# A ring of nine weight slots in place of six in the expert stage of a two-layer decoder trunk

## The reference

```python
def swiglu(x, w_gate, w_up, w_down):
    return (jax.nn.silu(x @ w_gate) * (x @ w_up)) @ w_down

def moe_swiglu(xn, w_router, we_gate, we_up, we_down):
    logits = (xn @ w_router).astype(jnp.float32)
    top_v, top_i = lax.top_k(logits, TOP_K)            # TOP_K = 2
    top_w = jax.nn.softmax(top_v, axis=-1)
    gates = jnp.sum(jax.nn.one_hot(top_i, N_EXPERTS, dtype=jnp.float32) * top_w[..., None], axis=-2)
    y = jnp.zeros_like(xn)
    for e in range(N_EXPERTS):                         # 8
        y = y + gates[..., e:e + 1].astype(xn.dtype) * swiglu(xn, we_gate[e], we_up[e], we_down[e])
    return y
```

## Time and profile before

| | us |
|---|---|
| median of 3 runs (range) | 1408.41 (1406.65 to 1410.0) |
| profiled execution, whole | 1407.37 |
| its span | 1405.5 |
| TensorE matmul busy | 1325.4 (94%) |
| VectorE busy | 779.1 (55%) |
| ScalarE busy | 680.1 (48%) |
| mean granted TensorE clock | 0.994 of full |
| moved by DMA | 442.34 MB, mean 315 GB/s |
| in the chain that ended last: TensorE / DMA | 66% / 25% |

### The profile page before, as it was taken

How to read it: one execution, slowest core, us unless ns; L and a number is a source line. 1 busy time by engine, 2 the same in 40 slices (tenths; PEclk the granted TensorE clock), 3 DMA queues, 4 the chain that set the end, 5 groups by cost and what they waited for, 6 DMA issues and landing times.

```text
span 1405.5 us, 18008 instructions
## 1 busy us (share of the span) xinstructions
PE 1325.4 (94%) x6371; PEld 904.1 (64%) x6371; DVE 779.1 (55%) x1123; ACT 680.1 (48%) x941; POOL 40.4 (3%) x109
## 2 busy tenths in 40 slices
PE   9999999999999999998889998889999889999886
PEld 8998888888897878841258871137884126886112
DVE  6968655544589699910069950029991006995100
ACT  6766544444479487710068850028871006874000
POOL 1000000000010000000000000000000000000000
PEclk9999999999999999999999999999999999999999
DMA  8654565555162599989999999999999999999997
GB/s 293 191 186 157 181 201 181 190 188 195 52 230 82 206 352 403 371 315 409 402 403 409 402 348 401 407 402 406 409 402 340 409 402 403 409 402 342 404 407 297
DMA packets 150198, 442.34 MB, mean 315 GB/s; under 512 B 15486, under 2 KB 27868, under 8 KB 150108
## 3 DMA queue, kind: packets, MB, share of 16 engines
q1 hardware_dynamic: 146796, 429.92, 81.0%
q0 software_dynamic: 3280, 11.27, 2.6%
q10 hardware_dynamic: 32, 0.01, 0.0%
HBM read 434.06 MB, written 7.08 MB: 314 GB/s over the span
## 4 chain that ended last, share of the span: by engine, by line
PE 66%; DMA 25%; DVE 5%; ACT 2%; issue 1%; SPq 0%; POOL 0%; DVEq 0%; ACTq 0%; POOLq 0%
PE bank L618 62%; DMA raw<-in_we_down_dram 10%; DMA raw<-in_we_gate_dram 8%; DMA raw<-in_we_up_dram 7%; DVE w_lo L2142 3%; DVE qkT L2265 1%; PE bank L1263 1%; ACT w_hi L1534 1%; SPq L391 0%; PE bank L963 0%; PE bank L630 0%; DVE xT_lo L2186 0%; ACT xr L1669 0%; PE bank L638 0%; PE bank L1227 0%
## 5 line engine op out<-in xcount | busy, mean ns | idle before, releaser
L2142 DVE TENSOR_TENSOR w_lo<-raw,w_hi 128x1024 fp32r<-128x1024 f32 (+3 forms) x496 | 565.4, 1182 | 136.3 <-ACT w_hi L1534 131.6
L1534 ACT ACTIVATE w_hi<-raw 128x1024 fp32r<-128x1024 f32 (+3 forms) x496 | 498.5, 1032 | 199.2 <-PE bank L618 153.5
L618 PE MATMUL bank<-w_hi,xT_hi 128*128 128x512 f32 (+4 forms) x910 | 351.7, 387 | 11.0 <-DVE w_lo L2142 9.6
L618 PE MATMUL bank<-w_hi,xT_lo 128*128 128x512 f32 (+4 forms) x910 | 346.4, 381 | 0.0
L618 PE MATMUL bank<-w_lo,xT_hi 128*128 128x512 f32 (+4 forms) x910 | 346.2, 380 | 0.0
L618 PE MATMUL bank<-raw,x_half 128*64 128x512 f32 (+1 forms) x1024 | 229.2, 561 | 34.9 <-DMA raw<-in_we_gate_dram 19.7
L618 PEld LDWEIGHTS bank<-w_hi,xT_hi 128*128 128x128 f32 x910 | 171.3, 188 | 47.8 <-issue 14.7
L2911 DVE SCALAR_TENSOR_TENSOR act_f<-bank,gslot,silu_g 128x512 f32<-128x512 f32 (+1 forms) x16 | 11.0, 684 | 331.4 <-PE bank L618 331.4
L618 PEld LDWEIGHTS bank<-w_hi,xT_lo 128*128 128x128 f32 x910 | 171.3, 188 | 31.4
L618 PEld LDWEIGHTS bank<-w_lo,xT_hi 128*128 128x128 f32 x910 | 171.5, 188 | 29.2
L618 PEld LDWEIGHTS bank<-raw,x_half 128*64 128x64 f32 x1024 | 60.5, 136 | 193.2 <-DMA raw<-in_we_gate_dram 72.6
(11 more groups left out here) (407 smaller groups left out, 813.5 us busy)
## 6 DMA issues: line engine op xcount, KB each, us to landing
raw<-in_we_gate_dram SPq DMA_DIRECT2D x224, 512.0 KB, 11.8
raw<-in_we_up_dram SPq DMA_DIRECT2D x224, 512.0 KB, 12.1
raw<-in_we_down_dram SPq DMA_DIRECT2D x224, 512.0 KB, 12.3
raw<-in_w_gate_dram SPq DMA_DIRECT2D x28, 512.0 KB, 4.3
raw<-in_w_up_dram SPq DMA_DIRECT2D x28, 512.0 KB, 4.3
raw<-in_w_down_dram SPq DMA_DIRECT2D x28, 512.0 KB, 4.0
raw<-in_w_in_dram SPq DMA_DIRECT2D x32, 384.0 KB, 4.8
raw<-in_w_out_dram SPq DMA_DIRECT2D x16, 512.0 KB, 5.5
```

The costliest lines, as they stand in the source:

```text
L618: return pe.matmul(o, a, b, start=start, stop=stop, skip_group_check=True, **kw)
L1534: act.activation(split_piece(w_hi, c, shape, half), raw_piece(c, shape, half), ACT.Copy).then_inc(hi_ready, 1)
L2142: dve.tensor_tensor(split_piece(w_lo, c, shape, half), raw_piece(c, shape, half), F(split_piece(w_hi, c, shape, half)), ALU.subtract).then ...
```

## The change

`RING = 9` slots serve the expert stage. Six of them are those of `raw`. Two more (`spare`) lie above the other buffers of the stage, and the ninth (`late_slot`) where `xT_lo` lay, which is now closed before the expert stage. The two parts of a wide unit's tokens both go into `xT_hi` (`xE`): the high part in the first half of its bytes, the low part in the second. The layers before the experts keep their ring of six.

A chunk that falls into one of the three new slots is fetched by one DMA of 1 MiB (`ring_piece` with `half=None`), which waits until both halves of the chunk before it in that slot are done with; both of its pieces count as landed only with the whole. In the first lap the two `spare` slots wait for the attention scores (`scores_psum`), the late one for TensorE's last product of the output projection (`piece_used` at 2*C_MOE).

```diff
+RING = 9
@@
-        xT_lo = sb("xT_lo", [P, KD, S], F32R)
...
+        before_moe = ExitStack()
+        xT_lo = sb("xT_lo", [P, KD, S], F32R, scope=before_moe)
...
+        before_moe.close()
         part = ExitStack()
         with part:
+            late_slot = sb("late_slot", [P, CHUNK], scope=part)
...
+            spare = sb("spare", [P, 2, CHUNK], scope=part)
@@
+        def place(u, c):
+            return divmod(c - C_MOE + FFN_CHUNKS * u, RING)
+        def ring_piece(u, c, shape, half):
+            s = place(u, c)[1]
+            slot = (raw[:, (C_MOE + s) % RAW_SLOTS, :] if s < RAW_SLOTS else
+                    spare[:, s - RAW_SLOTS, :] if s < RING - 1 else late_slot[:, :])
+            k0, nk = (0, shape[0]) if half is None else pieces_of(shape)[half]
+            return slot[:, k0 * shape[1]:(k0 + nk) * shape[1]].rearrange("p (k n) -> p k n", k=nk)
+        def ring_here(u, c, half):
+            lap, s = place(u, c)
+            if s < RAW_SLOTS:
+                return raw_here[2 * ((C_MOE + s) % RAW_SLOTS) + half], 16 * ((C_MOE + s) // RAW_SLOTS + 1 + lap)
+            return spare_here[s - RAW_SLOTS], 16 * (2 + lap)
@@
             def slot_free(u, c, half):
-                owner = u if c - RAW_SLOTS >= C_MOE else u - 1
-                n = 2 * (c - RAW_SLOTS + FFN_CHUNKS * u) + half + 1
-                if owner in NARROW_UNITS:
-                    sp.wait_ge(piece_used, n)
+                lap, s = place(u, c)
+                if lap:
+                    owner, i = divmod(RING * (lap - 1) + s, FFN_CHUNKS)
+                    if owner in NARROW_UNITS:
+                        sp.wait_ge(piece_used, 2 * (C_MOE + FFN_CHUNKS * owner + i) + half + 1)
+                    else:
+                        sp.wait_ge(lo_ready, 2 * (C_MOE + split_chunks(owner) + i) + half + 1)
+                elif s < RAW_SLOTS:
+                    sp.wait_ge(lo_ready, 2 * (c - RAW_SLOTS) + half + 1)
+                elif s < RING - 1:
+                    sp.wait_ge(sem("scores_psum"), AH)
                 else:
-                    sp.wait_ge(lo_ready, n - 2 * FFN_CHUNKS * (max(owner, 0) - wides_before(owner)))
+                    sp.wait_ge(piece_used, 2 * C_MOE)
+            def fetch_expert(u, c, shape, src):
+                s = place(u, c)[1]
+                if s < RAW_SLOTS:
+                    for half, (k0, nk) in enumerate(pieces_of(shape)):
+                        slot_free(u, c, half)
+                        sp.dma_start(ring_piece(u, c, shape, half), src[:, k0:k0 + nk, :]).then_inc(
+                            raw_here[2 * ((C_MOE + s) % RAW_SLOTS) + half], 16)
+                else:
+                    slot_free(u, c, 1)
+                    sp.dma_start(ring_piece(u, c, shape, None), src).then_inc(spare_here[s - RAW_SLOTS], 16)
@@
-                    dve.tensor_tensor(xT_lo[:, k, 0:P], B[b][:, :].rearrange("p (k s) -> p k s", k=4),
-                                      F(xT_hi[:, k, 0:P]), ALU.subtract).then_inc(sem("gather_ready"), 1)
+                    dve.tensor_tensor(xE[1][:, k, :], B[b][:, :].rearrange("p (k s) -> p k s", k=4),
+                                      F(xE[0][:, k, :]), ALU.subtract).then_inc(sem("gather_ready"), 1)
```

More of the change, by code:

```diff
@@ L295, in hybrid_trunk @@
         xT = (xT_hi, xT_lo)
+        xE = [flat3(xT_hi[:, :, :])[:, a * KD * P:(a + 1) * KD * P].rearrange("p (k s) -> p k s", k=KD) for a in range(2)]
         wS = (w_hi, w_lo)
@@ L381, in small_rows, with fetch @@
                 sp.dma_start(hnorm_bc[:, :], h_norm0.partition_broadcast(P)).then_inc(sem("bias_here"), 16)
-            def fetch(c, shape, src, more=0, unit=None):
+            def fetch(c, shape, src, more=0):
                 for half, (k0, nk) in enumerate(pieces_of(shape)):
-                    if unit is not None:
-                        slot_free(unit, c, half)
-                    elif c >= RAW_SLOTS:
+                    if c >= RAW_SLOTS:
                         sp.wait_ge(lo_ready, 2 * (c - RAW_SLOTS + more) + half + 1)
@@ L461, in down_rows @@
                     for j in range(2):
-                        fetch(c + j, DOWN, down[j, here, f:f + 1].rearrange("a b p k n -> (a b p) k n"), unit=u)
+                        fetch_expert(u, c + j, DOWN, down[j, here, f:f + 1].rearrange("a b p k n -> (a b p) k n"))
                 wide(c0, 0)
@@ L1237, in e_in @@
                         for a, b in TERMS:
-                            last = mm(B[which][:, :], xT[a][:, k, 0:P], w[b][:, i, :],
+                            last = mm(B[which][:, :], xE[a][:, k, :], w[b][:, i, :],
                                       start=(k == 0 and (a, b) == (0, 0)), stop=(k == KD - 1 and (a, b) == TERMS[-1]))
@@ L1356, in n_turn, with n_down @@
                 last.then_inc(sem("aT_psum"), 1)
-            def n_down(c, lap, n, blocks, start, stop, at0=0, inside=None):
+            def n_down(u, c, n, blocks, start, stop, at0=0, inside=None):
                 pe.wait_ge(sem("aT_hi_ready"), NF - 2 + n + 1)
@@ L1372, in next_gate @@
                 if u in NARROW_UNITS:
-                    n_in(C_MOE, 0, NF * u, gathered=2 * u)
+                    n_in(u, C_MOE, 0, gathered=2 * u)
                 else:
@@ L1521, in _, with split_high, split_expert_high @@
             done = [0]
-            def split_high(p, shape, more=0, lap=0, unit=None):
+            def split_high(p, shape, more=0, lap=0):
                 c, half = p // 2, p % 2
                 act.wait_ge(raw_here[2 * (c % RAW_SLOTS) + half], 16 * (c // RAW_SLOTS + 1) + 16 * lap)
-                if unit is not None:
-                    before = unit if p - SPLIT_SLOTS >= 2 * C_MOE else last_wide(unit) + 1
-                    act.wait_ge(piece_used, p - SPLIT_SLOTS + 1 + 2 * FFN_CHUNKS * before)
-                elif p >= SPLIT_SLOTS:
+                if p >= SPLIT_SLOTS:
                     act.wait_ge(piece_used, p - SPLIT_SLOTS + 1 + 2 * more)
                 act.activation(split_piece(w_hi, c, shape, half), raw_piece(c, shape, half), ACT.Copy).then_inc(hi_ready, 1)
+            def split_expert_high(u, p):
+                c, half = p // 2, p % 2
+                act.wait_ge(*ring_here(u, c, half))
+                before = u if p - SPLIT_SLOTS >= 2 * C_MOE else last_wide(u) + 1
+                act.wait_ge(piece_used, p - SPLIT_SLOTS + 1 + 2 * FFN_CHUNKS * before)
+                act.activation(split_piece(w_hi, c, WROW, half), ring_piece(u, c, WROW, half), ACT.Copy).then_inc(hi_ready, 1)
             def splits_to(p):
@@ L2939, in unit, with pieces @@
                 first = u == 0
-                def pieces(a, b, m=more):
+                def pieces(a, b, i=0):
                     for j in range(a, b):
-                        split_low(p0 + j, WROW, m)
+                        split_expert_low(u, p0 + j + 2 * WIDE_STEP * i)
                 pieces(6, 8)
```

71 lines of the change are left out of this document (38 added, 33 removed).

## The result

| | before | after |
|---|---|---|
| median | 1408.38 us (1406.65 to 1410.0) | **1382.97 us** (1381.51 to 1384.04) |
| ratio to before, 95% | | 0.9819 [0.9802, 0.9836] |
| profiled execution, its span | 1407.37, 1405.5 us | 1383.28, 1381.5 us |

The change takes off 25.4 us. I had forecast 1389.0 in 1383 to 1398, that is 18.8 us off the profiled execution. The direction and the mechanism held; the size was a quarter too small, and the time lies just outside the range, at its low end.

The account below looks back on a forecast made before the run. The prediction took the DMA to bound the stage, with TensorE waiting in narrow units. Gains of 7.7 and 11.1 us, 18.8 off the profiled 1407.37, gave 1388.6, with the median's offset 1389.6, stated as 1389.0; range 1383 to 1398.

Parts of the forecast that it names:

- What bounds the kernel: Expert stage: the DMA bounds it, 215 us per pair of units against TensorE's 197; TensorE waits in narrow units.
- Term 1: First change from wide to narrow, unit 1: starts with 18 pieces landed, not 12, and ends 7.7 us sooner.
- The price of TensorE's piece: Narrow units: TensorE takes 0.905 us for each 512 KB piece, read from 18 pieces in 16.29 us.
- Term 2: Three later changes from wide to narrow: the DMA no longer stands still, 3.6, 3.7 and 3.8 us, together 11.1 us.
- the price of a piece in a new slot: New slots: one 1 MiB DMA was taken to cost 2.56 us, as much as two streaming pieces of 1.28 us.
- Rival B: More comes back: gentle DMA restart at three changes, 1386; with whole chunks at 418 GB/s too, 1381; 13%.
- The only term on the tokens: Wide units: reading both token parts from one tensor instead of two costs 0, being 128 contiguous columns either way.
- a sign of slower splits or token reads: Wide units were forecast unchanged at 121.3 us; longer ones would mean that splits or token reads had got slower.
- C: Rival: only the later changes gain, since the ring isn't full at 607.5 us; 11.1 us off, 1397.5; 5%.
- D: Rival: only the first change gains, as the later gaps belong to the adding DMA; 7.7 us off, 1401; 5%.
- E: Rival: SP works in order and a new slot's wait holds the queue, so no change, 1408; 4%.
- F: Rival: slower, a whole chunk costs the stream more than two pieces; at 0.4 us more each, 1427; 5%.

## Why the prediction was too small

The runs make a ledger from before to after, by medians, each line one edit against the line above:

| | us | step |
|---|---|---|
| before | 1408.55 | |
| buffers moved, ring of six | 1412.17 | +3.6 |
| nine slots, spare ones at 128 modulo 256 | 1394.49 | -17.7 |
| spare slots at 0 | 1385.10 | -9.4 |
| whole chunks in the new slots | 1382.97 | -2.1 |

**What bounds the kernel: right.** Depth by itself gives 17.7 us where terms 1 and 2 made 18.8. The third line comes from another group of runs than its neighbours, whose kernel before is 0.4 us slower; taken each against its own, the steps around it are 18.1 and 9.0.

**Term 1: right.** Unit 1 went from 106.8 to 98.4 us, and to 98.2 with the spare slots at 128: 8.4 to 8.6 against 7.7. The traces have 12 pieces landed at its start before and 18 after, as forecast. The price of TensorE's piece, 0.905 us, was read too high, without harm to the sum: the 16.29 us of the earlier trace rows run past the twelve landed pieces and contain waits. Twelve rows take 2.575 us, so a piece takes 0.86.

**Term 2: right.** With the spare slots at 128 units 3, 5 and 7 are 4.6, 3.1 and 2.8 us shorter than before, 10.5 together against 11.1, and the stretch around the first of these changes has its rate back:

```profile
828.00:836.00 8.00, 8.00 (x38) 4.58 (x38) 0.00 (x0) 1.47 (x3) 1.58 (x1) 1.00 1.03 409
```

That two extra slots would do at the later changes was right as well: eight were expected at 1387.7 us and measured at 1387.62. The count behind it was less exact, and that the time fits so closely is partly luck. I took the ring of six for full and the DMA for stopped, and 14.8 of 18 for landed with nine. In the traces 10 or 11 of the 12 handed out have landed when units 3, 5 and 7 start (the fewest on their way around these starts are one, none and none), and with nine slots 12 or 13 of 18.

**Where it failed: the price of a piece in a new slot.** "Whether the DMA engines move it at the same rate I can't read" ended in "I take 2.56". I had put the question as one of size, one DMA of 1 MiB against two, and size is worth some 2.1 us. What changed the rate was the address: a piece landing in a spare slot, at 0 modulo 256, takes 1.235 us and not 1.28, and it made 9.0 to 9.4 us. Rival B had the right range of times, 1381 to 1386, for mostly the wrong reason, which is luck: it counted on whole chunks and on a gentle restart.

A rule was there to be read. "DMA: Bandwidth & Descriptors", section How a descriptor splits into AXI transactions, of the Trainium skill says that transfers go in transactions that start at multiples of 256 bytes, and that one which starts between two such addresses needs one more of them. It speaks of reads and doesn't say that it holds for a landing address. My estimate by it is that a row of 4 KB at 128 modulo 256 takes 132 beats for 128, 3.1% more; the runs show 410 against 420 GB/s, 2.4%. The direction agrees, and the step is near it. For the late slot at 192 the same working gives 134 beats, and there the agreement is poor: with nine slots and the spare ones at 0 its pieces land 1.289 us behind the one before, those of the old slots at 128 after 1.281. I had weighed the same page's numbers on rate and on size, and not asked where the new slots lie.

**Where it failed a second time, with the other sign.** The only term on the tokens was "Reading both token parts from one tensor instead of two I take as 0", from "128 contiguous columns either way". For the expert stage that nearly holds: with the buffers moved and six slots the wide units take 121.2, 121.8 and 121.7 us, and before they took 121.2, 121.3 and 121.7. So the 0.5 to 1.0 us by which the changed kernel's wide units are longer, which I had named as a sign of slower splits or token reads, don't come from the reads in two of the three; what they come from no run shows. Left out of the sum was that `xT_lo` has another address in the layers before: at 192 modulo 256 it costs 3.6 us there, 9 products in 450 in the stretch shown. I had looked only at the stage that the change is meant for; the token parts are read from the start of the program on.

**The other rivals didn't come.** All four changes gained (against C and D), the ring did what it says (E), and whole chunks cost the stream nothing (F).

**What stays open.** The gain isn't additive. Two slots of nine at 0 give 3 of the 10 GB/s, but by the time 9.4 of the some 22 us that all of them give. From 127 pieces behind the start of unit 1, 2/9 of 570, at 0.045 us I get 5.7 us and not 9.4. In the traces the stretch from unit 1 on is 771.0 us with them at 128 and 762.8 at 0, 8.2 apart. The landings tell where most of it comes from (steps over 1.45 us, the gaps, are left out): the mean step to a spare piece goes from 1.281 to 1.234 us, 5.5 us over 116 pieces, and that to a piece of the old slots, which haven't moved, from 1.286 to 1.281, 1.8 us over 357. And once nearly all land at 0, a piece takes 1.245 to 1.25 us and no longer 1.235. Why, no run tells. Only slots at 0, 128 and 192 modulo 256 were tried, and none of those at 0 lay at a multiple of 512. The old slots never moved alone: `w_hi`, `w_lo`, `h` and `xT_hi` moved with them.

What slows TensorE is not settled either. With `w_hi` and `w_lo` at 128 a product on a token part at 192 is slow each time. With them at 0 it isn't so plain: the steps behind products on `aT_hi` and `aT_lo`, still at 192, are 226 to 232 ns by kind, and those behind `xT_lo`, also at 192, 231. So it may be how the two operands lie to each other and not the address of one. No run separates these.

## What to carry to other kernels

Work out how deep a ring must be from what the DMA can bring in while the consumer is busy elsewhere: here an estimated 14.8 pieces, 12 or 13 by the traces, so that the seventh and eighth slot pay everywhere and the ninth once. When an edit moves buffers, list every address that it moves, modulo 256 bytes, for what lands there by DMA and for what TensorE reads from there, over the whole program and not just in the stage that is edited; here two such shifts were worth 9 us one way and 4 the other, and putting all at 0 another 16. An engine that still waits after the change isn't a sign against it: see whether the resource behind it runs dry.

## What the runs showed of the hardware

- Loads from HBM in rows of 4 KB stream into SBUF at 409 to 410 GB/s where they land at 128 (and the late slot at 192) modulo 256 bytes, at 419 to 420 where all or nearly all land at 0. The time of a packet goes from 163.2 to 159.3 ns.
- Neither the size of a DMA, 512 KB or 1 MiB, nor the number of 512 KB in flight, 6 or 11 to 13, moves the steady rate with the spare slots at 0: 412 to 414 GB/s in all of them.
- SP may hand out 18 pieces, but never more than 14 of 512 KB were on their way at once.
- With `w_hi` and `w_lo` at 128 modulo 256, a product of 128 by 512 is followed by the next after 227 ns where the token part, loaded as weights, is at 128 too, and after 233 to 236 ns where it is at 192. With both at 0 it is 226 to 227 ns, with the first at 0 and the token part at 192 it is 226 to 232. The granted clock is 1.00 in all of them.
- TensorE's own pace on landed float32 pieces of the old slots is 2.575 us for twelve rows of products with them at 128 and at 0.
